# Retention gate in two tiles of seven products, and the retention output kept token by token until it is turned

## The reference, cut to what matters

```
u = rms_norm(h);  proj = u @ w_in
aq, ak, av, rq, rk, rv, rg, gates = split(proj)
y_att = sliding_window_attention(rms_norm(aq), rms_norm(ak), av)      # 16 heads
y_ret = rms_norm(chunkwise_retention(rq, rk, rv)) * silu(rg)          # 4 heads of 256, norm per head and token
merged = sigmoid(g_att) * (y_att @ w_attn_branch) + sigmoid(g_ret) * (y_ret @ w_ret_branch)
h = h + merged @ w_out
h = h + moe_ffn(rms_norm(h))                                          # top 4 of 32 experts, clamped SwiGLU
```

## Time and profile before

| | us |
|---|---|
| median of 3 runs | 1225.26 (1225.15 to 1225.83) |
| the profiled execution's own time | 1226.07 |
| its span, first to last instruction | 1224.3 |

### The profile page before, as it was taken

The page is one execution under the profiler, slowest core; times in us unless marked ns, Lnnn a source line. Parts: engine busy times, 40 slices in busy tenths (PEclk is TensorE's granted clock), DMA queues, the critical chain, the costliest instruction groups (busy, mean ns, idle before and its releaser), DMA issues.

```text
span 1224.3 us, 14125 instructions
## 1 busy us (share of the span) xinstructions
PE 1147.9 (94%) x5723; PEld 627.0 (51%) x5723; DVE 361.7 (30%) x638; ACT 137.5 (11%) x274; POOL 8.2 (1%) x18
## 2 busy tenths in 40 slices
PE   9999999999999999989798998988888989898998
PEld 7878888888444353434343443434343535252433
DVE  4155357762214140312222121213040403030321
ACT  2233312011101010000001010101010100000001
POOL 1000001000000000000000000000000000000000
PEclk9999999999999999999999999999999999999999
DMA  8532344666999999999999999999999999999996
GB/s 331 204 104 103 109 166 191 240 242 264 391 426 425 427 428 428 427 428 428 428 428 428 429 428 428 428 429 428 428 429 429 429 428 429 429 429 428 423 421 277
DMA packets 40450, 446.75 MB, mean 365 GB/s; under 512 B 4288, under 2 KB 5952, under 8 KB 7392
## 3 DMA queue, kind: packets, MB, share of 16 engines
q1 hardware_dynamic: 39792, 443.89, 86.8%
q10 hardware_dynamic: 624, 2.38, 0.5%
HBM read 444.94 MB, written 1.05 MB: 364 GB/s over the span
## 4 chain that ended last, share of the span: by engine, by line
PE 66%; DMA 29%; DVE 2%; issue 2%; SPq 1%; ACT 0%; DVEq 0%; ACTq 0%
PE ps L1096 17%; DMA ring<-in_w_down 17%; PE ps L673 12%; DMA arena<-in_w_down 12%; PE ps L1119 10%; PE ps L711 7%; PE ps L1085 7%; PE ps L1053 5%; PE ps L1169 2%; DVE arena L1877 1%; PE ps L1105 1%; PE ps L1151 1%; PE ps L801 0%; PE ps L1114 0%; SPq L587 0%
## 5 line engine op out<-in xcount | busy, mean ns | idle before, releaser
L1096 PE MATMUL ps<-ring,arena 128*64 128x512 f32 x1216 | 272.2, 603 | 18.9 <-DMA ring<-in_w_gate_up 18.9
L1096 PEld LDWEIGHTS ps<-ring,arena 128*64 128x64 f32 x1216 | 92.6, 139 | 191.1 <-issue 191.1
L1119 PE MATMUL ps<-ring,arena 128*64 128x512 f32 x672 | 150.4, 600 | 26.0 <-DMA ring<-in_w_down 24.6
L673 PE MATMUL ps<-arena,ring 128*128 128x256 f32 (+1 forms) x672 | 154.8, 385 | 0.0
L1859 DVE COPY arena<-ps 128x1024 f32<-128x1024 f32 x16 | 19.6, 1224 | 426.0 <-PE ps L1096 376.7
L673 PEld LDWEIGHTS ps<-arena,ring 128*128 128x128 f32 x672 | 124.7, 189 | 24.7 <-issue 5.0
L1096 PE MATMUL ps<-arena 128*64 128x512 f32 x448 | 103.7, 617 | 13.8 <-DMA arena<-in_w_gate_up 13.8
L1119 PEld LDWEIGHTS ps<-ring,arena 128*64 128x64 f32 x672 | 55.0, 138 | 116.5 <-issue 116.5
L1852 DVE TENSOR_TENSOR arena<-ps,arena 128x512 f32<-128x512 f32 x64 | 41.1, 683 | 144.0 <-PE ps L1105 144.0
L1475 ACT ACTIVATE arena<-ps 128x1024 f32<-128x1024 f32 x16 | 16.4, 1023 | 570.0 <-PE ps L1096 499.8
L711 PE MATMUL ps<-ring 128*128 128x256 f32 x352 | 78.9, 380 | 0.7 <-DVE arena L1664 0.7
(11 more groups left out here) (247 smaller groups left out, 736.1 us busy)
## 6 DMA issues: line engine op xcount, KB each, us to landing
ring<-in_w_gate_up SPq DMA_DIRECT2D x94, 2048.0 KB, 26.9
ring<-in_w_down SPq DMA_DIRECT2D x47, 2048.0 KB, 24.7
arena<-in_w_gate_up SPq DMA_DIRECT2D x33, 2048.0 KB, 26.9
ring<-in_mix_w SPq DMA_DIRECT2D x36, 1024.0 KB, 4.9
arena<-in_w_down SPq DMA_DIRECT2D x16, 2048.0 KB, 24.7
ring<-in_w_down SPq DMA_DIRECT2D x2, 1024.0 KB, 30.4
arena<-in_consts ACTq DMA_DIRECT2D x1, 1552.0 KB, 12.6
arena<-in_xT SPq DMA_DIRECT2D x2, 544.0 KB, 4.4
```

The costliest lines, as they stand in the source:

```text
L673: last = mm(ps[:, PROJ + BANK[c], 0:rhs.shape[-1]], w[:, k, half * P:(half + 1) * P], rhs, start=(k == 0), stop=(final and k == features[- ...
L1096: last = mm(ps[half, bank + b], columns[:, j, half], w[x][:, at:at + 512], start=(j == 0), stop=(j == 7))
L1119: return mm(ps[halves[x], DOWN + b], e_act[:, k, halves[x]], w[:, j * D + b * 512:j * D + (b + 1) * 512], start=(k == 0), stop=(k == 7))
```

## The change

The gate `rg` becomes two tiles of seven products and stays token-major (`rg_tok`). There are now ten tiles, two more than before, and the loop's chunks 8 to 15 are replaced by 14 products in pairs ("slots" 8 to 14, in place of 15 chunks and one behind). DVE reads them in the same places where it read the chunks (`slot_read`), with `last_sum` behind P6, and makes the sums of weights for three tiles in passes 1 to 7. Retention's output has tokens on partitions, so a head's sum of squares runs along the free side: ACT's squares add up by themselves, one root and one reciprocal serve all heads, `ret_out` does root and gate in one instruction per head and block, POOL's adds and the products with ones are gone, and PE turns the gated output 16 times (`turn_y`), with four copies by ACT back into the same place. The sums of `wr`'s input wait for these copies. The third 2 MB unit of the experts waits for P4 of the second `gr` tile where it waited for P3.

```diff
-TILES = (("ga", 0), ("wa", 0), ("ga", 1), ("wa", 1), ("gr", 0), ("wr", 0), ("gr", 1), ("wr", 1))
-TILED = ("ga", "wa", "gr", "wr")
+TILES = (("rg", 0), ("rg", 1), ("ga", 0), ("wa", 0), ("ga", 1), ("wa", 1), ("gr", 0), ("wr", 0), ("gr", 1), ("wr", 1))
+TILED = ("rg", "ga", "wa", "gr", "wr")
...
-            return cut((in_tmp, in_p, in_p, in_p, in_att, in_att, in_att, in_norm)[n], 0, (4, TOK))
+            return cut((in_tmp, in_tmp, in_tmp, in_p, in_p, in_p, in_att, in_att, in_att, in_norm)[n], 0, (4, TOK))
 
         def gated(n):
-            return cut({5: in_att, 7: in_norm}[n], 1024, (2, 2 * TOK))
+            return cut({7: in_att, 9: in_norm}[n], 1024, (2, 2 * TOK))
 
         def tile_operand(kind):
-            return u_norm if kind in ("ga", "gr") else attT if kind == "wa" else rgT
+            of = u_norm if kind in ("rg", "ga", "gr") else attT
+            return yT if kind == "wr" else of.rearrange("p k (b t) -> p k b t", b=2)
...
-            for h in range(RH):
-                pool.wait_ge(ret_sq, h + 1)
-                half = sq[:, h % 2, 0:TOK]
-                nc.gpsimd.tensor_tensor(half, half, sq[:, h % 2, TOK:2 * TOK], ALU.add).then_inc(ret_halved, 1)
-
...
-                sp.wait_ge(proj_done, AT[("gr", 1, P3)] + 1)
+                sp.wait_ge(proj_done, AT[("gr", 1, P4)] + 1)
...
+                for b in range(2):
+                    for h in range(RH):
+                        mm(ps[:, ret_bank(h), b * RDV:(b + 1) * RDV], rs_meta[quarter(h), b * BLK:(b + 1) * BLK],
+                           rv_meta[quarter(h), h * RDV:(h + 1) * RDV], start=(b == 0), stop=False, skip_group_check=True)
+
+            def retain(h):
+
+                f = slice(h * RDV, (h + 1) * RDV)
+                for b in range(2):
+                    o = ps[:, ret_bank(h), b * RDV:(b + 1) * RDV]
+                    last = mm(o, rs[:, h, b * BLK:(b + 1) * BLK], rv_tok[:, 0, f], start=False, stop=(b == 0),
+                              skip_group_check=True)
+                    if b == 1:
+                        last = mm(o, rs[:, h, TOK:TOK + BLK], rv_tok[:, 1, f], start=False, stop=True, skip_group_check=True)
+                last.then_inc(ret_done, 1)
+
+            def turn_y(h):
+
+                pe.wait_ge(ret_ready, h + 1)
                 for v in range(2):
-                    for h in range(RH):
-                        f = slice((2 * h + v) * P, (2 * h + v + 1) * P)
-                        mm(ps[:, ret_bank(h), v * TOK:(v + 1) * TOK], rv_meta[quarter(h), f], rs_meta[quarter(h)],
-                           start=(v == 0), stop=False, skip_group_check=True)
-
-            def retain(h):
-
-                bank = ret_bank(h)
-                for v in range(2):
-                    f = slice((2 * h + v) * P, (2 * h + v + 1) * P)
-                    o = ps[:, bank, v * TOK:(v + 1) * TOK]
-                    mm(o, rv_tok[:, 0, f], rs[:, h, 0:TOK], start=False, stop=False, skip_group_check=True)
-                    last = mm(o[:, BLK:TOK], rv_tok[:, 1, f], rs[:, h, TOK:TOK + BLK], start=False, stop=True,
-                              skip_group_check=True)
-                last.then_inc(ret_done, 1)
-
-            def ret_stats(h):
-                pe.wait_ge(ret_halved, h + 1)
-                bank = PT_META + h % 2
-                if h >= 2:
-                    pe.wait_ge(ret_root, h - 1)
-                mm(ps[:, bank, 0:TOK], ones, sq[:, h % 2, 0:TOK], start=True, stop=True).then_inc(ret_stat, 1)
+                    for b in range(2):
+                        at = (2 * h + v) * P
+                        last = turn(ps[:, PT_META + h, (2 * v + b) * BLK:(2 * v + b + 1) * BLK], rg_tok[:, b, at:at + P], ident)
+                last.then_inc(y_turned, 1)
...
+            def slot(i):
+
+                if i < 8:
+                    whole(AT[("rq", 0)] + i)
+                else:
+                    for j in (2 * (i - 8), 2 * (i - 8) + 1):
+                        multiply("rg", j // GROUPS, j % GROUPS)
+
             for i in range(1, PAIRS - 1):
-                c = AT[("rq", 0)] + 2 * i + 1
-                whole(c)
+                slot(2 * i + 1)
                 turn_probs(i - 1)
-                whole(c + 1)
+                slot(2 * i + 2)
                 attend(i - 1)
                 if i + 1 < PAIRS:
                     scores(i + 1)
-            whole(AT[("rg", KC - 1)])
...
-            for kind, t in TILES[3:7]:
+            for g in (P6, P7, P5, P3, P4, P2):
+                multiply("ga", 1, g)
+            for g in (P1, P6, P7):
+                multiply("wa", 1, g)
+            turn_y(0)
+            turn_y(1)
+            multiply("wa", 1, P5)
+            multiply("wa", 1, P3)
+            turn_y(2)
+            turn_y(3)
+            multiply("wa", 1, P4)
+            multiply("wa", 1, P2)
+            for kind, t in (("gr", 0), ("wr", 0), ("gr", 1)):
...
             def ret_square(h):
                 act.wait_ge(ret_done, h + 1)
                 if h >= 2:
-                    act.wait_ge(ret_stat, h - 1)
-                A(sq[:, h % 2], ps[:, ret_bank(h)], ACT.Square).then_inc(ret_sq, 1)
-
-            def ret_sqrt(h):
-                act.wait_ge(ret_stat, h + 1)
-                if h >= 1:
-                    act.wait_ge(ret_ready, h)
-                A(root[:, 0:TOK], ps[:, PT_META + h % 2, 0:TOK], ACT.Sqrt, bias=const("eps"),
-                  scale=1.0 / RDV).then_inc(ret_root, 1)
+                    act.wait_ge(ret_sq, 2 * (h - 1))
+                for b in range(2):
+                    A(sq[:, h % 2, b * RDV:(b + 1) * RDV], ps[:, ret_bank(h), b * RDV:(b + 1) * RDV], ACT.Square,
+                      accum_out=ret_sums[:, h, b:b + 1]).then_inc(ret_sq, 1)
+
+            def y_copy(h):
+                act.wait_ge(y_turned, h + 1)
+                A(yT[:, 2 * h:2 * h + 2], ps[:, PT_META + h].rearrange("p (v b t) -> p v b t", v=2, b=2),
+                  ACT.Copy).then_inc(y_copied, 1)
...
+            act.wait_ge(ret_sq, 2 * RH)
+            A(ret_roots, ret_sums, ACT.Sqrt, bias=const("eps"), scale=1.0 / RDV).then_inc(ret_root, 1)
...
+            def slot_read(i):
+
+                c = AT[("rq", 0)] + i
+                if i < 8:
+                    evict(c, place_of(c))
+                    return
+                for j in (2 * (i - 8), 2 * (i - 8) + 1):
+                    if j < 2 * GROUPS:
+                        combine("rg", j // GROUPS, j % GROUPS)
+                        if j % GROUPS == P6:
+                            last_sum(j // GROUPS)
...
+            for i in range(PAIRS):
+                slot_read(2 * i)
...
+                bias_scores(i)
+                slot_read(2 * i + 1)
+                normalise(i)
+                if i in (1, 2, 3):
+                    sum_weights(0, i - 1)
+                elif i == 4:
+                    sum_weights(1, 0)
+                    sum_weights(1, 1)
+                elif i == 5:
+                    sum_weights(1, 2)
+                elif i == 6:
+                    sum_weights(2, 0)
+                    sum_weights(2, 1)
+                elif i == 7:
+                    sum_weights(2, 2)
...
             def ret_out(h):
 
                 bank = (SCORE, SCORE + 1, PT + 1, PV)[h]
-                rr = tmp[:, 0, 0:TOK]
-                g = rgT[:, 2 * h:2 * h + 2]
-                link(V.tensor_tensor(g, g, rr.rearrange("p (o t) -> p o t", o=1).to_broadcast([P, 2, TOK]), ALU.mult))
-                V.tensor_tensor(g, g, ps[:, bank].rearrange("p (v t) -> p v t", v=2), ALU.mult).then_inc(ret_ready, 1)
+                for b in range(2):
+                    g = rg_tok[:, b, h * RDV:(h + 1) * RDV]
+                    last = V.scalar_tensor_tensor(g, ps[:, bank, b * RDV:(b + 1) * RDV], ret_recs[:, h, b:b + 1], g,
+                                                  ALU.mult, ALU.mult)
+                last.then_inc(ret_ready, 1)
...
+            combine("ga", 1, P6)
+            last_sum(4)
+            combine("ga", 1, P7)
+            dve.wait_ge(ret_root, 1)
+            link(V.reciprocal(ret_recs, ret_roots))
             ret_out(0)
```

## The result

The changed kernel takes 1237.72 us (median of 4 runs, 1237.06 to 1238.0) against 1225.55 (4 runs): a ratio of 1.0098, 95% interval 1.0086 to 1.011. It is 12.2 us slower. Its profiled execution took 1237.06 us, its span is 1235.2.

The account below looks back on a forecast made before the run. PE's time up to the mixer's end was taken as the bound, since the experts' transfers start from there. Terms -3.4 - 0.6 + 12.4 + 3.4 = +11.8 us on 1225.26 gave 1237.0 us; range 1229 to 1240.5.

Parts of the forecast that it names:

- What starts the transfers: Experts' stage: its transfers wait for the mixer's last product, so the kernel's end moves with it, us for us.
- rival D: Experts' stage: units sent early let it catch up, so the delay is swallowed and nothing changes, 1225; chance 0.04.
- PE's own work: PE up to the mixer's end: fewer matmuls and no products with ones, less sixteen added turns; -3.43 us.
- The loop: Attention loop: six PE waits on DVE's reads and sums, 13.0 us where 0.65 stood; +12.4 us, bounds 8 and 14.
- Retention: PE's wait behind DVE at the second `wa` tile shrinks from 1.28 to 0.7 us; -0.6 us, bounds -1.3 and 0.
- The clock: Behind the loop's two waits over 4 us the granted clock falls to half; 2 x 1.69 = +3.4 us, bounds 0 and 3.4.
- Transfers: Third early expert unit goes out one product (1.73 us) later, covered by 9 us of DMA idle time; 0.
- A: In the loop the waits come but the clock falls once or not at all: 1235.4 or 1233.7 us; chance 0.20.
- B: In the loop the waits are about half as long, DVE or ACT being faster: about 1228 to 1230; chance 0.10.
- E: Retention's new chain is late too, or the clock stays low longer: +14 to +17, 1239 to 1242; chance 0.07.
- C: In the loop DVE does sums and reads during ACT's exponentials, no waits: 4.7 us gained, 1220.6; chance 0.04.

Follow-up runs that it names:

- delay of known size: The kernel before with 20 unused matmuls of 128x256 (8.6 us of PE) behind the second `gr` tile: 1234.15 us, ratio 1.0069 to before.
- sums and reads first: Changed kernel, sums of passes 1 to 7 ahead of `normalise`, reads of P1 and P6 of first `ga` tile ahead of the last one: 1221.36 us.
- the half alone: Retention as in the changed kernel, but token-major `rg` made by plain multiplication, eight chunks without sums: 1224.87 us, ratio 0.9992 to before.
- the fillers: Changed kernel with 10 and 9 unused matmuls of 128x240 put into PE's two long waits in the loop: 1233.38 us, ratio 1.0063 to before.
- third sum earlier: Changed kernel with the third sum of weights of the second `rg` tile made one pass earlier: 1233.65 us, ratio 1.007 to before.

## Why the prediction was right

The forecast was 1237.0 us, the measured time is 1237.72. Its steps:

**What starts the transfers.** Right: the delay of known size came through whole, rival D falls.

**PE's own work**, -3.4. Right. With the sums and reads first the mixer ends 3.58 us earlier than before. Its two waits in the loop hold PE up for 0.37 and 0.66 us, the old one did for 0.73; the wait at the second `wa` tile holds it up for 0.84 where it was 1.44 (the way of counting is told under "The loop"). That makes 3.58 + 0.30 - 0.60 = 3.28 for the work. The 0.15 that is missing is about what two products behind a wait take more: 3.53 or 3.56 us from their start to the next instruction, others 3.46.

**Retention**, -0.6: measured 1.28 to 0.67, and 0.5 us for the half alone. The single-bank hand-over between two tiles was the right reason why the wait did not vanish: in the changed kernel DVE waits for PE's last product there, reads it, and PE goes on 0.56 us after the read begins, at 221.09.

```profile
220.53 0.42 DVE L1663 TENSOR_TENSOR arena<-arena,ps 128x256 f32<-128x256 f32 x1 [0.52 <-PE ps L709]
```

**The loop**, term by term. The trace's brackets count idle time from the end of the last matmul. The forecast counts from the moment at which the next could have started, which is earlier, since rows of matmuls overlap (a product's row is 1.89 us long, the next instruction starts after 1.73). The last column counts in the forecast's way:

| wait of PE | forecast | idle in the trace | held up |
|---|---|---|---|
| P7 of the first `rg` tile | 0.95 | 0.89 | 0.95 |
| P3 | 0.6 | 0.40 | 0.57 |
| P2 | 1.55 | 1.38 | 1.45 |
| P7 of the second tile (third sum) | 4.5 | 4.32 | 4.48 |
| P1 of `ga` | 1.3 | 1.11 | 1.28 |
| P7 of `ga` (read of P1) | 4.1 | 4.04 | 4.10 |
| together | 13.0 | 12.14 | 12.83 |

The fourth, for example: the product ahead starts at 108.50, the next could have started at 108.50 + 1.73 = 110.23, and it started at 114.71. So each wait was forecast to 0.1 us. The moments at which PE goes on agree too. From the end of one wait to the end of the next the forecast had 5.05, 7.24, 10.7, 16.2 and 8.9 us; the rows above give 96.83 - 91.86 = 4.97, then 7.24, 10.64, 17.79 and 8.96, and in the fourth the 1.5 us of the slow clock are contained. Laying the queues side by side could be this exact because every duration came from rows of the same instructions in the same program, and only their order was new. The wait of before, put at 0.65, was 0.73 in this way of counting.

**The clock**, +3.4: measured 1.5 + 1.7 = 3.2 in the trace, 3.1 removed by the fillers. The mechanism was right. That both falls came was a bet on rows at 2.7 us, where the clock fell about half the time; with one fall the time would have been some 1.6 us shorter.

**Transfers**, 0: right. The DMA engines are idle from 310 to 315 us in the changed kernel too, so the unit that is sent one product later costs nothing.

**Sum of the traced terms**: 12.83 - 0.73 + 3.2 - 0.60 - 3.28 = +11.4, and the mixer ends 11.4 us later. All terms but the last are from the changed kernel's trace; the work is from the trace with the sums and reads first.

**Rivals.** A (clock falls once or not at all) fell with the trace. B and E fell with the six waits. C, the faster case, was priced at 1220.6 us for a DVE that does its sums and reads while ACT does exponentials. The written order forbade it, so it did not come; written so, it came at 1221.36. That price, too, was a sum of rows, but part of the agreement is luck: C's 4.7 us are 3.6 in the trace, since 0.69 us of idle time stay in the loop where C has none. Retention's part of E had no wait to show. Two prices are a little off by their own terms: B's +2 to +4 us on the median of 1225.26 gives 1227.3 to 1229.3 and not 1228 to 1230, and the forecast's +11.8 gives 1237.1. Neither changes a reading.

## What to carry to other kernels

An edit that makes work on the bounding engine smaller can cost more than it saves. Here it did two things at once: with two PSUM banks and half-size products PE's lead over its reader shrank from two chunks of 3.46 us to two products of 1.73, and DVE got sums of weights to make for the new products, behind `normalise`. No run has the one without the other. The smaller lead alone is not the loss, though: with the sums and reads in the better order the same small products leave 0.69 us of idle time in the loop, and the longest wait (4.32 us) was for a sum and not for a bank. Look then not at how busy the reader is (DVE was idle 3.7 us in a pass) but at what stands behind its waits in the queue: work that doesn't need what the wait is for belongs ahead of it. And before a change is judged, price the same instructions in the best order; here 16 us lay between two orders of one set of instructions.

## What the runs showed of the hardware

TensorE's granted clock fell to its lower level behind each of four idle stretches of 4.0 to 4.3 us: two in the changed kernel, one in the kernel with the third sum earlier, and one in the experts' stage of the delayed kernel, where 32 matmuls then took 9.87 us:

```profile
547.16 9.87 PE L1122 MATMUL ps<-ring,arena 128*64 128x512 f32 x32 [4.21 <-DMA ring<-in_w_down]
```

It fell behind one of 3.38 us (kernel with the waits filled, experts' stage) and behind 62 of 117 waits of 2.6 to 2.7 us (experts' stage, all eight traces; 7 of 15 in the kernel before). It didn't fall in the loops behind one of 2.52 us, one of 1.95 or the shorter ones. Four of four is too few for a rule.

A fall cost 1.4 to 1.7 us of matmuls, 2.8 in the row above (7.09 us at full clock). In the experts' stage of the kernel before the falls cost nothing: rows behind a wait of 2.7 us start at 646.17, 704.90, 763.63, 822.37 and 881.09 us, 58.7 us apart, though the first three ran into a fall and the last two didn't.

Two `ACTIVATE` per head with a sum at their side, where one stood before, made no wait of PE, since products of another tile stand beside them. The sixteen turns of 128x128 are PE's own work, 1.76 us.
